# Expert rows regrouped by token quarter: the V sums move to TensorE's four column groups, the dots read PSUM

## What is computed

```python
def peer_ffn(x, w_q, sub_keys, u_tab, v_tab):
    q = (xf @ w_q).reshape(t, PEER_HEADS, 2, PEER_DKEY // 2)
    scores = jnp.einsum('thpd,hpnd->thpn', q, sub_keys)
    s_top, i_top = lax.top_k(scores, PEER_TOPK)
    ...
    best, pos = lax.top_k(cand, PEER_TOPK)
    expert_idx = jnp.take_along_axis(cand_idx, pos, axis=-1)
    gates = jax.nn.softmax(best, axis=-1)
    ...
        hid = gelu(jnp.einsum('td,thkd->thk', x_blk, u_tab[idx_blk]))
        coef = g_blk * hid
        return jnp.einsum('thk,thkd->td', coef, v_tab[idx_blk])
```

## Time and profile before

| | |
|---|---|
| median of three runs | 4173.53 us (4168.82 to 4189.53) |
| span of the profiled execution | 4065.6 us |
| the median less that span | 107.9 us |
| VectorE busy | 2832.9 us, 70% |
| GpSimd busy | 2533.7 us, 62% |
| TensorE busy | 2484.2 us, 61% |
| ScalarE busy | 670.3 us, 16% |
| moved by DMA | 1296.79 MB, mean 319 GB/s |
| granted TensorE clock, mean | 0.775 of 2.4 GHz |

### The profile page before, as it was taken

One profiled execution on the slowest core, in us unless ns is written; L12 is line 12 of the kernel. 1 busy time (PEld: TensorE's weight loads), 2 busy tenths in 40 slices (PEclk: granted clock), 3 DMA queues, 4 the chain that ended last, 5 costly groups with the idle time before them and its releaser, 6 DMA issues.

```text
span 4065.6 us, 29120 instructions
## 1 busy us (share of the span) xinstructions
PE 2484.2 (61%) x7326; PEld 1341.5 (33%) x7326; DVE 2832.9 (70%) x5396; ACT 670.3 (16%) x1466; POOL 2533.7 (62%) x2067
## 2 busy tenths in 40 slices
PE   6654458795686147877487335869468523873057
PEld 3432333343343133333333223334334222331023
DVE  2437885669848986567965797477974798567863
ACT  2310111111211102112121101121121111110011
POOL 0005686467745887366873787547774688747776
PEclk8776768896798558988588656989679756886589
DMA  8146999899997889889898889969999888978999
GB/s 283 56 141 263 346 314 388 295 356 359 339 389 278 289 307 357 326 296 400 302 374 319 286 299 353 386 245 377 346 338 376 287 294 310 377 290 287 365 409 356
DMA packets 400926, 1296.79 MB, mean 319 GB/s; under 512 B 38174, under 2 KB 82724, under 8 KB 397932
## 3 DMA queue, kind: packets, MB, share of 16 engines
q0 software_dynamic: 294912, 1073.87, 72.2%
q1 hardware_dynamic: 97772, 183.35, 12.4%
q10 hardware_dynamic: 8064, 37.58, 2.3%
HBM read 1280.42 MB, written 14.23 MB: 318 GB/s over the span
## 4 chain that ended last, share of the span: by engine, by line
PE 29%; DVE 22%; POOL 19%; issue 15%; DMA 9%; ACT 3%; DVEq 1%; SPq 0%; ACTq 0%; PEldq 0%; POOLq 0%; PEld 0%
POOL ring L370 19%; PE acc L686 13%; PE work L699 11%; DVE ring L950 4%; DMA wring<-in_peer_wq 4%; DMA wring<-in_w_in 3%; DVE proj L975 3%; DVE proj L971 2%; DVE hbuf L963 2%; PE work L672 2%; DMA ring<-in_peer_v,idxU 1%; ACT arena L400 1%; DMA ring<-in_peer_u,idxU 1%; PE work L819 1%; PE work L663 1%
## 5 line engine op out<-in xcount | busy, mean ns | idle before, releaser
L370 POOL DMA_INDIRECT ring<-in_peer_u,idxU x1024 | 1410.4, 1377 | 781.4 <-issue 355.4
L686 PE MATMUL acc<-ring,diag 128*128 128x512 f32 x2240 | 1084.7, 644 | 526.1 <-ACT diag L421 495.5
L370 POOL DMA_INDIRECT ring<-in_peer_v,idxU x896 | 951.7, 1062 | 665.3 <-DVE hbuf L963 258.0
L950 DVE CUSTOM_DVE_ANT_0 ring<-ring,n2U 128x1024 f32<-128x1024 f32 x1024 | 1203.3, 1222 | 105.0 <-DMA ring<-in_peer_u,idxU 94.4
L686 PEld LDWEIGHTS acc<-ring,diag 128*128 128x128 f32 x2240 | 457.4, 207 | 1145.8 <-issue 947.2
L963 DVE SCALAR_TENSOR_TENSOR hbuf<-ring,coefV,hbuf 128x1024 f32 (+1 forms) x464 | 596.3, 1285 | 260.2 <-DMA ring<-in_peer_v,idxU 176.0
L699 PE MATMUL work<-wring,nT 128*128 128x512 f32 (+1 forms) x1408 | 640.7, 609 | 80.8 <-DMA wring<-in_w_in 40.2
L699 PEld LDWEIGHTS work<-wring,nT 128*128 128x128 f32 x1408 | 279.8, 203 | 420.9 <-issue 336.4
L421 ACT ACTIVATE diag<-ident,coefV 128x128 f32<-128x128 f32 x560 | 184.5, 391 | 675.3 <-PE acc L686 521.6
L672 PE MATMUL work<-arena 128*128 128x128 f32 x768 | 144.2, 357 | 219.8 <-issue 205.5
L971 DVE MAX8 proj<-proj 128x8 f32<-128x128 f32 x256 | 51.0, 278 | 300.5 <-ACT proj L400 300.5
(11 more groups left out here) (219 smaller groups left out, 2065.6 us busy)
## 6 DMA issues: line engine op xcount, KB each, us to landing
wring<-in_w_in SPq DMA_DIRECT2D x80, 898.0 KB, 14.4
wring<-in_peer_wq SPq DMA_DIRECT2D x64, 1024.0 KB, 15.6
wring<-in_w_out SPq DMA_DIRECT2D x32, 1024.0 KB, 17.8
ring<-in_peer_u,idxU POOLq DMA_INDIRECT x1024, 6.3
ring<-in_peer_v,idxU POOLq DMA_INDIRECT x896, 6.4
par<-par_scr ACTq DMA_DIRECT2D x8, 1184.0 KB, 7.0
arena<-keys_scr ACTq DMA_DIRECT2D x8, 1024.0 KB, 8.3
proj<-proj_scr ACTq DMA_DIRECT2D x3, 1796.0 KB, 10.8
```

The source lines that it names most:

```text
L370: nc.gpsimd.indirect_dma_start(ring[:, s * D:(s + 1) * D], None, table, bass.IndirectOffsetOnAxis(ap=idx, axis=0)).then_inc(row_in[s], 16)
L686: ins = nc.tensor.matmul(acc[c][:], diag[:, d * P:(d + 1) * P], ring[:, s * D + 512 * c:s * D + 512 * c + 512], start=(m == 0 and r == 0), ...
L950: V.tensor_tensor_reduce(out=rw, in0=rw, in1=n2U[:], scale=1.0, scalar=0.0, op0=ALU.mult, op1=ALU.add, accum_out=hid[:, kk:kk + 1]).then_i ...
```

## The change

**Rows by quarter.** A gather no longer fetches expert k of 128 tokens, but four experts of 32 tokens: partition 32o + p of column 4j + q holds expert 32o + j of token 32q + p. VectorE rewrites indices and coefficients into that order, 16 copies and 16 products of 32x32 (`rows_by_quarter`, `coefs`). `idxR` serves all V gathers, the last four units' too, so `idxT` goes.

**Sums by TensorE alone.** The weights of a slot are now 128x32: ScalarE scales `stack`, four 32x32 identities on top of each other, by the coefficients (`coef_blocks`), into one of four buffers of a unit. A matmul contracts 128 rows (32 tokens x 4 experts) to 32 tokens and writes 32 partitions of a bank, so the four slots of a unit go to four column groups of the array. A unit is eight matmuls behind one wait for all four rows, and one semaphore increment. `row_v`, VectorE's part, goes, and with it the numbers of `V_PLAN` that shared the rows out.

**Dots read PSUM.** The two banks of the sums are one tensor `accs` of 1024 columns. After the sums of the pair before were read (`sums_in`, now one instruction), `place_n2` copies the normed tile into them, and the dots take it from there until the V sums of this pair begin.

```diff
-PE_TAKES = [rows for _, v, rows in V_PLAN for _ in range(v)]
-PE_DONE = [sum(PE_TAKES[:q]) for q in range(NU + 1)]
-DVE_DONE = [UNIT * q - PE_DONE[q] for q in range(NU + 1)]
+QUARTER = P // UNIT
+WBUFS = 4
...
-                if kind == "V" and n == 0:
-                    pool.wait_ge(idxT_ready, t - 1)
+                if kind == "V" and n == SLOTS:
+                    pool.wait_ge(idxR_ready, t)
...
-                        pool.wait_ge(usedV, pe_count(tt, before[2] + 1))
-                        pool.sem_inc(drained_tick, 1)
-                        pool.wait_ge(usedVd, dve_count(tt, before[2] + 1))
+                        pool.wait_ge(usedV, units_v(tt, before[2] + 1))
...
-            def diags(t, first, q):
-                if q >= 2 and not (first and q < SLOTS + 2):
-                    act.wait_ge(usedV, pe_count(t, q - 1))
+            def coef_blocks(t, first, q):
+                if not (first and q < SLOTS + WBUFS):
+                    act.wait_ge(usedV, units_v(t, q + 1 - WBUFS))
                 if q == SLOTS:
                     act.wait_ge(S["coef_ready"], 1)
-                for r in range(PE_TAKES[q % NU]):
-                    d, kk = (UNIT - 1) * (q % 2) + r, UNIT * unit_of(q) + r
-                    nc.scalar.activation(diag[:, d * P:(d + 1) * P], ident[:], ACT.Copy, scale=coefV[:, kk:kk + 1]).then_inc(S["diag_ready"], 1)
+                for r in range(UNIT):
+                    d, kk = UNIT * (q % WBUFS) + r, UNIT * unit_of(q) + r
+                    nc.scalar.activation(wv[:, d * QUARTER:(d + 1) * QUARTER], stack[:], ACT.Copy, scale=coefR[:, kk:kk + 1]).then_inc(S["blocks_ready"], 1)
...
-                for r in range(PE_TAKES[q]):
-                    d, s = (UNIT - 1) * (q % 2) + r, UNIT * (pos % SLOTS) + r
-                    pe.wait_ge(S["diag_ready"], PE_DONE[q] + r + 1 - (PE_DONE[SLOTS] if first else 0))
-                    pe.wait_ge(row_in[s], row_count(t, pos))
-                    for c in range(2):
-                        ins = nc.tensor.matmul(acc[c][:], diag[:, d * P:(d + 1) * P], ring[:, s * D + 512 * c:s * D + 512 * c + 512],
-                                               start=(m == 0 and r == 0), stop=(m == NU - 1 and r == PE_TAKES[q] - 1))
-                    ins.then_inc(usedV, 1)
+                pe.wait_ge(S["blocks_ready"], UNIT * (q + 1 - (SLOTS if first else 0)))
+                for r in range(UNIT):
+                    pe.wait_ge(row_in[UNIT * (pos % SLOTS) + r], row_count(t, pos))
+                for c in range(2):
+                    for r in range(UNIT):
+                        d, s = UNIT * (q % WBUFS) + r, UNIT * (pos % SLOTS) + r
+                        ins = nc.tensor.matmul(acc[c][quarter(r), :], wv[:, d * QUARTER:(d + 1) * QUARTER], ring[:, s * D + 512 * c:s * D + 512 * c + 512],
+                                               start=(m == 0), stop=(m == NU - 1))
+                ins.then_inc(usedV, 1)
...
-                    V.tensor_tensor_reduce(out=rw, in0=rw, in1=n2U[:], scale=1.0, scalar=0.0, op0=ALU.mult, op1=ALU.add,
+                    V.tensor_tensor_reduce(out=rw, in0=rw, in1=accs[:], scale=1.0, scalar=0.0, op0=ALU.mult, op1=ALU.add,
                                            accum_out=hid[:, kk:kk + 1]).then_inc(usedU, 1)
-            def row_v(t, first, q, pos):
...
-                    if u and not first and b == 0:
-                        sums_in(j)
+                    if u and b == 0:
+                        if not first:
+                            sums_in(j)
+                        place_n2()
+                        rows_by_quarter()
...
+            def place_n2():
+                link(V.tensor_copy(accs[:], n2U[:]))
...
             def coefs():
                 dve.wait_ge(S["gelu_ready"], 1)
-                link(V.tensor_tensor(coefV[:], hid[:], gateU[:], ALU.mult), "coef_ready")
+                for q in range(UNIT):
+                    for o in range(UNIT):
+                        ins = V.tensor_tensor(regroup(coefR[:])[quarter(o), q, :], hid[quarter(q), quarter(o)], gateU[quarter(q), quarter(o)], ALU.mult)
+                link(ins, "coef_ready")
+            def rows_by_quarter():
+                for q in range(UNIT):
+                    for o in range(UNIT):
+                        ins = V.tensor_copy(regroup(idxR[:])[quarter(o), q, :], idxU[quarter(q), quarter(o)])
+                ins.then_inc(idxR_ready, 1)
...
-                    if gathered:
-                        dve.wait_ge(usedV, pe_count(t, NU))
-                        dve.sem_inc(met, 1)
```

67 lines of the change are left out of this document (29 added, 38 removed).

## The result

The changed kernel took **4210.65 us** (median of four runs, 4201.57 to 4223.01), the kernel before 4171.17 us beside it (4163.11 to 4189.53). The ratio is **1.0109, interval 1.0069 to 1.015: slower by 1.1%**, where 3978 us and a gain were forecast.

The account below looks back on a forecast made before the run. The bound changes by stretch: VectorE in dots and top-k, DMA in V sums. Terms -77 -20 -56 -18 -70 +24 +21 = -196 us give span 3870, time 3978 us, range 3860 to about 4090.

Parts of the forecast that it names:

- The base: Whole run: the median, 4173.53 us, lies 107.9 us above the profiled span, 4065.6, for what lies around it; left unchanged.
- VectorE loses its V rows: Top-k: nine V rows leave VectorE's path, so each of seven steps ends 11 us earlier, -77 us in all.
- Start: Step start: faster last four V units against added copies; -3.5 us in six steps and tail, +4 in first; -20 us.
- Column groups: V sums on TensorE: four groups run side by side, so a unit costs 1.9 us, 3.7 at the lower clock.
- Rival 1: V sums: the column groups run one after another, a unit costs 7.3 us; 4638 us in all, chance 0.09.
- The dots read PSUM: Dots: same price, but GpSimd no longer held up; -8 us a step, -56 us, and -18 us in the tail.
- rival 4: Dots: a dot from PSUM is slower; each 0.1 us costs up to 102 us, then 4080 us; chance 0.04.
- V sums up to the top-k: V sums before the top-k: DMA bounds; units gathered ahead and freed sooner win 10 us a step, -70 us.
- Clock: TensorE, less busy in V sums, may start a first product at the lower clock: 3 us a step, +21 us.
- rival 2: TensorE's products fall to the lower clock, six of 7.1 us a step double; 4257 us, chance 0.02.
- Rival 3: Whole step: only VectorE's part is won, V sums stay 153 us, rows come late in dots; 4083 us, chance 0.15.
- The side "slower": Whole run: chance 0.11 of a loss, from column groups running in turn (0.09) and products at the lower clock (0.02).

Follow-up runs that it names:

- first kind: Chips 0, 7 and 8, where the unchanged kernel before takes 4046 to 4054 us; the whole change, run there on chip 7 only, has ratio 0.9481.
- second kind: Chips 1 and 6, where the unchanged kernel before takes 4157 to 4196 us; the whole change has ratios 1.0285 and 1.0193 there.
- V part alone: Changed kernel with the dots reading the normed tile from SBUF as before; ratios to the kernel before 0.957 (chip 0), 0.9599 (chip 7), 0.9592 (chip 8).
- drain variant: Changed kernel, but a unit is counted as used by a drain of TensorE, not its last matmul; 3838.8 us on chip 0, 4270.3 us on chip 6.

## Why the prediction was wrong, point by point

Forecast and measured by the same parts, us over all steps: on the first kind the changed kernel of chip 7 less before of chip 0 (the medians of before there differ by 0.2%), on the second both of chip 6. The spans of the latter, 4240.2 and 4126.4, differ by 114, their medians by 80: the profiled execution of before was the fastest of its ten.

| part | forecast | first kind | second kind |
|---|---|---|---|
| top-k, 7 | -77 | -84 | -55 |
| start, 8 | -20 | -38 | -21 |
| dots, 7 | -56 | -37 | **+134** |
| tail dots | -18 | -12 | -4 |
| V sums with coefficients and clock, 7 | -70 + 21 + 21 = -28 | -61 | **+74** |
| tail V sums | +3 | -6 | -15 |
| step 0 | 0 | -2 | 0 |
| sum | -196 | -240 | +114 |

Parts of one kernel vary between executions too: against the profile that the prediction read, and not chip 0's, the first kind's dots would be -48, its tail dots -22 and its V sums -40, with the sum at -242. So the total is firm to a few us, and what lies in one part to some 20.

The stretches of the changed kernel on chip 7 (start, dots, V sums, top-k of step 5, tail):

```profile
2134.40:2158.30 23.90, 10.77 (x82) 4.35 (x82) 7.43 (x25) 6.36 (x20) 13.17 (x14) 0.71 0.96 356
2158.30:2361.80 203.50, 59.64 (x264) 51.69 (x264) 197.58 (x333) 25.74 (x45) 131.05 (x130) 0.55 0.91 339
2361.80:2512.50 150.70, 109.65 (x514) 44.06 (x514) 22.52 (x71) 38.54 (x123) 76.59 (x81) 0.83 0.98 376
2512.50:2567.20 54.70, 21.67 (x144) 5.04 (x144) 53.73 (x211) 9.41 (x38) 33.43 (x32) 0.71 0.83 305
3489.20:3650.10 160.90, 0.00 (x0) 0.00 (x0) 154.87 (x256) 0.00 (x0) 121.26 (x130) 0.50 1.03 410
3650.10:3824.00 173.90, 94.52 (x512) 19.76 (x512) 4.62 (x19) 30.27 (x129) 110.12 (x118) 0.67 0.98 389
```

- *The base.* "The median of the runs, 4173.53, is 107.9 us above, for what lies around the span" is the first wrong step. 1.8 us lie around it; the rest was most likely another chip. The forecast was in effect one for the profiled chip's kind: 3870 us of span, measured 3824 there. This step alone would have left a gain of 4.7%; the sign was lost in the dots and the V sums.
- *VectorE loses its V rows.* Right: top-k 54.7 us on the first kind, DMA share 0.83, VectorE 53.73 of it busy, and 12 us a step won of the 11 forecast. On the second kind 59 to 63, since VectorE there idles for up to 9 us of it.
- *Start.* Right in sign, and undersized on the first kind: from the second step on the first dot comes 5.5 to 7.8 us earlier than in before, for the 3.5 forecast, and 5 us later in the first, for 4.
- *Column groups.* Right: 16 records in 1.92 us at the upper clock. Rival 1 falls.
- *The dots read PSUM.* The dot's price was right (1217 ns; rival 4 falls; the 62 cycles of the Trainium skill, VectorE: DVE Perf Modes, TRN2 errata, do not show in this dot), and so was the end of the hold on GpSimd. "Rows will come in time, so -8 us a step" held on the first kind (203.5 us for 209.5 in step 5). On the second it is the step that failed most, +134 us for -56: no row of the profile read showed what full queues do beside TensorE there. Its ends, 3 and 13, both of one sign, left that out.
- *V sums up to the top-k.* "DMA bounds, so bytes decide" held on the first kind (share 0.98), and the gain (-61, or -40 by the other profile, with what was to be given back) was more than the 28 forecast. The 16 products of the coefficients take 207 ns each, so they add 3 us a step, as forecast. How the rest splits between V sums and clock no run shows. On the second kind DMA no longer bounds: its share falls from 0.99 to 0.85 in step 5 on chip 6, and the V sums take 74 us more than before, for 28 less. TensorE's late results lie there; that they are what costs it is argued.
- *Clock.* The granted clock fell in the tail's V sums from 0.93 to 0.71 (0.70 on chip 6, 0.67 on chip 7, so it is not what tells the kinds apart), and the products kept theirs (L701 at 610 ns a record, 609 before): rival 2 falls.
- *Rival 3* (only VectorE's part is won) is nearest to what the second kind shows, and for another reason. The side "slower" held 0.11, on two mechanisms that did not come; the one that did was not among them. The result's profile is what the section on what would show it named as wrong: engines that end waits on TensorE in the V sums. In the range's low end V sums stand at 12 us a step, where their own term gave 14; that is 14 us in all and changes nothing here.

**Shown**: the sign goes with the chip, on the three on which the whole change ran; late results are TensorE being held; VectorE is held as well; both go when the gathers are paced, on the same chip; the dots' part brings those of the dots. **Argued only**: that the V part brings those of the V sums, from halving TensorE's share (301 to 105 us). **Open**: what holds the engines, for no row names it, and whether it is something that they share, such as the way in which instructions reach them (no run tries it); what sets the two kinds apart; and how the V part alone fares on the second kind. The Trainium skill (TensorE: Matmul & The Clock Gate, Seeing it yourself) describes a current limiter that lowers the clock once three cores of a die run dense matmuls and not for one or two; here one core runs and the granted clock stays at its two levels, so by that page it is not this, and no run here tries it. No correct variant beats both kernels: the changed kernel is best on the first kind (its drain variant is as fast), before on the second.
